# Spreading RMS-norm reciprocals with fp32 matmuls, summing the last squares on TensorE, and pairing two units tile by tile

## The reference

```python
mod = (silu(c) @ ada_w + ada_b).reshape(b, 9, 1024)        # shifts, scales and gates
h = modulate(rmsnorm(x, norm_ffn1_g), sh1, sc1)
x = x + 0.5 * g1 * swiglu(h, ffn1_w1, ffn1_w3, ffn1_w2)    # D_FF = 2816
h = modulate(rmsnorm(x, norm_mix_g), sh2, sc2)
xb, xc, xu, cq, ckv, kr = split(h @ w_in)
y_a = short_conv_mixer(xb, xc, xu, conv_w)
y_b = mla(cq, ckv, kr, ...)                                # norms of cq and ckv, 4 heads, 128x128 blocks
y = concat(group_rmsnorm(y_a, 8 groups), group_rmsnorm(y_b, 4 heads)) @ w_out
x = x + g2 * y
h = modulate(rmsnorm(x, norm_ffn2_g), sh3, sc3)
x = x + 0.5 * g3 * swiglu(h, ffn2_w1, ffn2_w3, ffn2_w2)
return rmsnorm(x, final_norm_g)
# rmsnorm(x, g) = x * rsqrt(mean(x * x) + EPS) * g
```

## Time and profile before

| what | value |
|---|---|
| runs of the kernel | 1052.28, 1052.82, 1054.54 us |
| span of the profiled execution | 1052.8 us; no further time of that execution is given |
| instructions | 13254 |
| mean granted TensorE clock | 0.974 |

### The profile page before, as it was taken

How to read it: one execution, slowest core, us unless ns; L and a number is a source line. 1 busy time by engine, 2 the same in 40 slices (tenths; PEclk the granted TensorE clock), 3 DMA queues, 4 the chain that set the end, 5 groups by cost and what they waited for, 6 DMA issues and landing times. The chain is left out here.

```text
span 1052.8 us, 13254 instructions
## 1 busy us (share of the span) xinstructions
PE 1009.5 (96%) x4505; PEld 831.4 (79%) x4505; DVE 564.9 (54%) x754; ACT 400.6 (38%) x568; POOL 66.3 (6%) x79
## 2 busy tenths in 40 slices
PE   3699999999999999999999989999999999999997
PEld 3678888888888888888867777788888888888886
DVE  5868777787753333754377645744434333333332
ACT  3254434444332222442255443353444444332222
POOL 2411111011000000000000310000000000000000
PEclk9599999999999999999999799999999999999999
DMA  9547766687633324123221101223323333333232
GB/s 333 175 133 249 242 198 211 206 256 235 202 92 93 92 90 115 50 81 100 80 65 40 41 23 58 80 80 100 98 85 96 99 100 100 94 93 93 90 109 81
DMA packets 176622, 127.82 MB, mean 121 GB/s; under 512 B 5069, under 2 KB 165718, under 8 KB 176598
## 3 DMA queue, kind: packets, MB, share of 16 engines
q1 hardware_dynamic: 168534, 98.14, 31.1%
q0 software_dynamic: 8064, 29.36, 8.4%
HBM read 125.39 MB, written 2.10 MB: 121 GB/s over the span
## 5 line engine op out<-in xcount | busy, mean ns | idle before, releaser
L722 PE MATMUL pb<-hh,wh 128*128 128x512 f32 x912 | 358.5, 393 | 5.0 <-DVE hl L1159 2.8
L722 PE MATMUL pb<-hh,wl 128*128 128x512 f32 x912 | 355.8, 390 | 0.0
L722 PE MATMUL pb<-hl,wh 128*128 128x512 f32 x912 | 355.7, 390 | 0.0
L1118 DVE TENSOR_TENSOR wl<-raw,wh 128x1024 fp32r<-128x1024 f32 x156 | 191.1, 1225 | 275.1 <-ACT wh L408 275.0
L408 ACT ACTIVATE wh<-raw 128x1024 fp32r<-128x1024 f32 x163 | 172.5, 1059 | 410.5 <-PE pb L722 410.5
L722 PEld LDWEIGHTS pb<-hh,wh 128*128 128x128 f32 x912 | 171.5, 188 | 46.5 <-DVE hl L1159 7.2
L722 PEld LDWEIGHTS pb<-hh,wl 128*128 128x128 f32 x912 | 171.6, 188 | 36.2
L722 PEld LDWEIGHTS pb<-hl,wh 128*128 128x128 f32 x912 | 171.7, 188 | 34.5
L722 PE MATMUL pb<-gh,wh 128*128 128x512 f32 x352 | 137.0, 389 | 0.0
L722 PE MATMUL pb<-gh,wl 128*128 128x512 f32 x352 | 136.9, 389 | 0.0
L722 PE MATMUL pb<-gl,wh 128*128 128x512 f32 x352 | 136.9, 389 | 0.0
(11 more groups left out here) (193 smaller groups left out, 763.2 us busy)
## 6 DMA issues: line engine op xcount, KB each, us to landing
raw<-in_ffn_w_dram SPq DMA_DIRECT2D x104, 512.0 KB, 3.8
ada_ring<-in_ada_w_dram POOLq DMA_DIRECT2D x56, 512.0 KB, 5.1
raw<-in_ffn_w_dram SPq DMA_DIRECT2D x32, 448.0 KB, 3.4
raw<-in_w_in_dram SPq DMA_DIRECT2D x17, 512.0 KB, 3.9
ada_start<-in_ada_w_dram SPq DMA_DIRECT2D x8, 1024.0 KB, 16.4
raw<-in_w_out_dram SPq DMA_DIRECT2D x8, 512.0 KB, 3.4
x_nat<-in_x_dram SPq DMA_DIRECT2D x1, 2048.0 KB, 10.5
out_dram<-o_nat SPq DMA_DIRECT2D x8, 256.0 KB, 2.9
```

The costliest lines, as they stand in the source:

```text
L722: last = pe.matmul(o, a, b, start=start and j == 0 and t == 0, stop=stop and j == len(pairs) - 1 and t == 2)
L1118: dve.tensor_tensor(wl[par][:, :], raw[par][:, :], wh[par][:, :].bitcast(F32), ALU.subtract).then_inc(lo_ready, 1)
```

## The change

Four things change. `inverse` only computes the reciprocals, after a wait until the spread before has been done (TensorE now reads `rrms` itself); the split parts, `diag` and their semaphores are gone. `norm_spread` is four fp32 matmuls, one for each column of reciprocals: the column, repeated 128 times, is the stationary operand and the identity is the moving one, 128 columns. For the norms of mix, FFN2 and the final one, `norm_sum_last` sums `sacc` of seven tiles and then the eighth square straight from its slot of `sq`, so that VectorE doesn't add it. `first_pair` uses each tile for both units at once. The filler counts change, and `fold` no longer waits for the first spread, since `turned` has its own place. The other lines renumber the count of additions (`ADD_BASE`).

```diff
-LAG = 3
-WARM_START, WARM_SQUARES, WARM_ROOT, WARM_NORMED, WARM_HEADS = 7, 16, 13, 16, 9
+WARM_START, WARM_SQUARES, WARM_ROOT, WARM_NORMED, WARM_HEADS = 7, 4, 3, 13, 9
...
+            def norm_sum_last(n, slot, applied):
+
+                pe.wait_ge(u_ready, applied)
+                pe.wait_ge(sq_added, ADD_BASE[n] + DT - 1)
+                for t in range(TT):
+                    pe.matmul(norm_bank[:, t:t + 1], cols(sacc, t), one_col, start=t == 0, stop=False, skip_group_check=True)
+                pe.wait_ge(sq_ready, SQ_BASE[n] + DT)
+                for t in range(TT):
+                    last = pe.matmul(norm_bank[:, t:t + 1], cols(sq[:, slot, :], t), one_col, start=False, stop=True, skip_group_check=True)
+                last.then_inc(col_done, 1)
...
             def norm_spread(n):
 
-                for part in range(2):
-                    pe.wait_ge(diag_ready, 2 * n + part + 1)
-                    last = pe.matmul(norm_bank[:, :], exact[:, 0, :], diag[:, part, :, :], start=part == 0, stop=part == 1)
+                pe.wait_ge(rrms_ready, n + 1)
+                for t in range(TT):
+                    last = pe.matmul(cols(norm_bank, t), rrms[:, t:t + 1].to_broadcast([P, P]), ident, start=True, stop=True)
                 last.then_inc(bc_done, 1)
...
-                for k in range(DT + LAG):
-                    for b, kb in ((0, k), (1, k - LAG)):
-                        if not 0 <= kb < DT:
-                            continue
-                        if kb == 0:
+                for k in range(DT):
+                    for b in range(2):
+                        if k == 0:
                             unit(base + b)
...
             warm(WARM_SQUARES)
-            pe.wait_ge(sq_added, SQ_BASE[N_MIX] + DT)
-            norm_sum(N_MIX, sacc, AP_BASE[N_MIX])
+            norm_sum_last(N_MIX, (SQ_BASE[N_MIX] + DT - 1) % 2, AP_BASE[N_MIX])
             warm(WARM_ROOT)
...
             def inverse(n, spread=True):
 
                 dve.wait_ge(rms_ready, n + 1)
+                if n >= 1:
+                    dve.wait_ge(bc_done, SPREAD[n] if spread else SPREAD[N_FFN2] + 1)
                 dve.reciprocal(rrms[:, :], rms[:, :]).then_inc(rrms_ready, 1)
-                dve.wait_ge(rrms_ready, n + 1)
                 if not spread:
-                    return
-                dve.tensor_copy(rrms_h[:, :], rrms[:, :]).then_inc(rrms_split, 1)
-                dve.wait_ge(rrms_split, 2 * n + 1)
-                dve.tensor_tensor(rrms_l[:, :], rrms[:, :], rrms_h[:, :].bitcast(F32), ALU.subtract).then_inc(rrms_split, 1)
-                if n >= 1:
-                    dve.wait_ge(bc_done, SPREAD[n])
-                idb = ident.unsqueeze(1).to_broadcast([P, TT, P])
-                for part, r in enumerate((rrms_h[:, :].bitcast(F32), rrms_l[:, :])):
-                    dve.wait_ge(rrms_split, 2 * n + part + 1)
-                    dve.tensor_tensor(diag[:, part, :, :], idb, r.unsqueeze(2).to_broadcast([P, TT, P]),
-                                      ALU.mult).then_inc(diag_ready, 1)
+                    dve.wait_ge(rrms_ready, n + 1)
```

More of the change, by code:

```diff
@@ L157, in hybrid_block @@
                                            ("group_rl", [P, SEQ], F32R))
-        diag_at = top[0]
-        diag = at("diag", [P, 2, TT, P], F32R)
-        (turned,), _ = place(diag_at, ("turned", [P, D_MODEL], F32))
+        turned = at("turned", [P, D_MODEL])
         region = top[0]
@@ L411, in landed, with square @@
                 return 16 * (n // 2 + 1)
-            def square(idx, slot, src):
-                if not isinstance(idx, int) or idx >= 2:
-                    act.wait_ge(sq_added, idx - 1)
+            def square(n, j, slot, src):
+                if n != N_FFN1 or j >= 2:
+                    act.wait_ge(sq_added, ADD_BASE[n] + j - 1)
                 act.activation(sq[:, slot, :], src, ACT.Square).then_inc(sq_ready, 1)
@@ L471, in _ @@
                 act.wait_ge(x_copied, k + 1)
-                square(k, k % 2, xres[:, k, :])
+                square(N_FFN1, k, k % 2, xres[:, k, :])
             sqrt_table(6)
@@ L507, in _ @@
                     act.wait_ge(zkv_copied, j + 1)
-                    square(SQ_BASE[N_KV] + j, (SQ_BASE[N_KV] + j) % 2, zkv[:, j, :])
+                    square(N_KV, j, (SQ_BASE[N_KV] + j) % 2, zkv[:, j, :])
                 elif j < KT + QT:
@@ L512, in _ @@
                     act.wait_ge(zq_copied, q + 1)
-                    square(SQ_BASE[N_Q] + q, (SQ_BASE[N_Q] + q) % 2, zq[:, q, :])
+                    square(N_Q, q, (SQ_BASE[N_Q] + q) % 2, zq[:, q, :])
                 if j == KT:
@@ L532, in conv_square @@
                 act.wait_ge(yc_ready, FREE + j + 1)
-                act.wait_ge(sq_added, SQ_BASE[N_Q] + QT)
+                act.wait_ge(sq_added, ADD_BASE[N_Q] + QT)
                 if j >= 2:
@@ L676, in _ @@
                         act.wait_ge(x_upd, DT + d + 1)
-                        square(SQ_BASE[N_FFN2] + d, (SQ_BASE[N_FFN2] + d) % 2, xres[:, d, :])
+                        square(N_FFN2, d, (SQ_BASE[N_FFN2] + d) % 2, xres[:, d, :])
                 if last:
@@ L757, in first_pair @@
             def first_pair(base, hbase):
[L759 to L763 removed]
+                for k in range(DT):
+                    for b in range(2):
+                        if k == 0:
                             unit(base + b)
[L765 to L768, removed]
+                        pe.wait_ge(hl_ready, hbase + k + 1)
+                        last = three(pb[b][:, :], [(cols(wh[b], k), cols(wl[b], k), hh[:, k, :], hl[:, k, :])],
+                                     k == 0, k == DT - 1)
+                        if k == DT - 1:
                             last.then_inc(unit_done, 1)
@@ L1079, in _ @@
             warm(WARM_SQUARES)
-            pe.wait_ge(sq_added, SQ_BASE[N_FFN2] + DT)
-            norm_sum(N_FFN2, sacc, AP_BASE[N_FFN2])
+            norm_sum_last(N_FFN2, (SQ_BASE[N_FFN2] + DT - 1) % 2, AP_BASE[N_FFN2])
             warm(WARM_ROOT)
@@ L1248, in update, with down_pair @@
                                          op0=ALU.mult, op1=ALU.add).then_inc(x_upd, 1)
-            def down_pair(base, f, n, upd, m, splits=6):
+            def down_pair(base, f, n, upd, m, splits=6, sums=2):
                 for s in range(6):
@@ L1255, in down_pair @@
                         update(d, 2 + p, half_gates[:, f, bass.ds(d, 1)], base + 6 * m + s + 1, upd)
-                        add_square(n, SQ_BASE[n] + 2 * m + p, (SQ_BASE[n] + p) % 2)
+                        if p < sums:
+                            add_square(n, 2 * m + p, (SQ_BASE[n] + p) % 2)
                     if s < splits:
@@ L1337, in _ @@
             clear_sum(N_MIX, N_FFN1)
-            with dve.Fori(0, DT // 2) as m:
+            with dve.Fori(0, DT // 2 - 1) as m:
                 down_pair(U_B1, 0, N_MIX, 0, m)
+            down_pair(U_B1, 0, N_MIX, 0, DT // 2 - 1, sums=1)
             inverse(N_MIX)
```

38 lines of the change are left out of this document (17 added, 21 removed).

## The result

The changed kernel took 1061.3 us (median of 1058.50, 1061.23, 1061.37 and 1061.41) against 1053.1 us for the kernel before (1052.28 to 1054.54, four runs): ratio 1.0074, 95% interval 1.0060 to 1.0088. It is 8 us slower. The forecast was 1053.1 with a range of 1049.0 to 1056.8, and the measured time lies 4.5 us beyond its upper end. The profiled execution is the one of 1058.50 us, its span 1056.8.

The account below looks back on a forecast made before the run. TensorE, busy 96% of the span, was taken as the bound. Terms -2.4 - 1.7 + 1.5 + 0.9 + 0.3 + 0 + 0 + 1.7 = +0.3 on 1052.8 gave 1053.1 us, range 1049.0 to 1056.8.

Parts of the forecast that it names:

- Second head, -2.4 - 1.7: Second head: without `diag` TensorE's stall goes, -2.4 us, and the half-clock stretch after it, another -1.7.
- Spreads, +1.5: KV, Q and heads: four fp32 matmuls cost TensorE 0.48 us more per spread in a stream, together +1.5 us.
- Last addition, mix 0: Mix norm: dropping the last addition gains 0, because `split_lo` of the next unit still holds the reciprocal.
- Final, +0.9: Final norm: two groups of sums stand behind the transposes in place of one, moving the end by +0.9 us.
- Start, +0.3: Kernel's start: half-clock spread replaces the `diag` wait, first tile at half clock for both units; +0.3 us.
- Clock at the norms, 0 and 0: Mix and FFN2 norms: fewer fillers let the clock fall, cancelling the shorter spread's gain; 0 us each.
- Pairs without lag, one fall, +1.7: First pairs: 0 by time, but TensorE's stands before unit 2 bring one clock fall among three places, +1.7 us.
- three falls: Rival: the clock falls behind all three first pairs, giving 1056.5 us; chance 0.22.
- The base: Starting time: the profiled execution's span of 1052.8 us was taken to stand for the runs' median of 1052.82.

Follow-up runs that it names:

- the changed kernel with the 64 bytes: Changed kernel plus 64 unused bytes a partition ahead of the region of `gh` and `gl`, restoring their old addresses; 1053.9 us, 1.0006 of the kernel before.
- bench1: Kernel before plus 512-column matmuls at varied operand addresses behind its last transposes; no total time given, final root at 1042.49 against 1044.22.

## Why the prediction was wrong

**The step that failed is one that it doesn't have.** The change frees `rrms_h` and `rrms_l`, and the prediction gives that no line. By moving `gh` and `gl` against the weights it costs 7.4 us, and 1053.1 + 7.4 = 1060.5 is within 1 us of what was measured. The forecast for the rest, without the addresses, was 1053.1; measured 1053.9. That is in part luck, since terms were missed on both sides; each is compared below, in the profile of the changed kernel with the 64 bytes against the profile of before.

- *Second head, -2.4 - 1.7*: right, -4.1 (reciprocal to reciprocal 10.53 us before, 6.45 here; the same with the spread alone). By the Trainium skill, "SBUF — State Buffer", section Who interferes with whom, a VectorE instruction with one SBUF input, outside the two-port modes, isn't held by GpSimd's; the trace agrees: in the changed kernel the reciprocal takes 0.18 us at 627.39, in the middle of a `wl` of GpSimd.
- *Spreads, +1.5*: right, 0.89 for 0.45 in a stream (forecast 0.93). By the Trainium skill, "FP8 and Floating Point Precision", section TensorE Precision Notes, true fp32 takes four passes; the estimate from that was 0.85 us, and the trace is 0.04 from it.
- *Last addition, mix 0*: right, `split_lo` bounds the reciprocal (423.69 against 423.82). *Final, +0.9*: right, 0.8.
- *Start, +0.3*: measured -0.2.
- *Clock at the norms, 0 and 0*: the mechanism was right at mix in this profile. The clock fell at 424.80, `ubuf` started 1.14 us earlier than before, 13 fillers took 4.04 us, and unit 0 was done at 439.23 against 439.25: nothing is left of the gain. At FFN2 it was mis-sized: unit 0 came 1.7 us later, since the second group of sums and the spread ran at half clock too (1.47 and 1.91 us). In the changed kernel's own profile the mix norm kept 1.00, and there 1.2 us were gained at `ubuf`. Of the four kernels with few fillers ahead of the sums one profile has the fall at mix (this one), and all four have it at FFN2 (3.4 us long in the two with the lag, 6.8 in the others).
- *Pairs without lag, one fall, +1.7*: mechanism and price of a fall right, the number too low. I gave three falls 0.22; the profiles have two here (1.7 and 1.4 us), three in the kernel before without lag, none in the changed kernel. By time the missing lag costs 0 to 0.3 us a pair where 0 was forecast.
- *Not foreseen*: in the first head the stretches at 0.50 are 10.2 us long in place of 17.1, and 1.6 us less are lost on the path. It isn't the length that counts: the spread alone and the pairs without lag, both on the kernel before, have 10.2 us too and gain nothing. These two have the fall early in the head (from 574.7 and 577.3) as before has (574.2), and this profile hasn't. As `bench1` hasn't it either, it takes no change for it to be missing; whether the change makes it rarer, these profiles don't tell.
- *The base*: a profiled execution's time is its span and 1.7 us (1058.50 for 1056.8, 1055.56 for 1053.9). That of before took some 1054.5, not 1052.8, so the prediction was wrong to let its span stand for the median. It joined the rows of an execution with a fall at 574, which `bench1` lacks, to the median of the others. The fall behind the second head, on which the -1.7 rests, is in every profile with `diag`.

## What to carry to other kernels

A deleted buffer is an edit to every address behind it: print both memory plans, compare them, and put a spacer in before anything else is judged. Where TensorE is the bound, check that moving and stationary operands have the same remainder by 256 (measured here for 512-column fp32r matmuls alone). Where a wait is shortened, shorten the fillers that were sized for it. Of a change that brings stands of 2 us in front of long matmul streams expect falls of the clock, whatever one profile shows; and before two profiles are compared, list the falls that each has.

## What was unexpected of the hardware

- The spacing of 512-column fp32r matmuls depends on the difference of their two operands' addresses by 256: 227 to 229 ns for 0, 229 to 230 for the moving one 64 ahead, some 232 to 235 for the other six steps of 32, with all other engines idle; 226.0, 228.2 and 232.7 in the down stages (the two windows by their 948 matmuls).
- The three stands of 1.8 to 2.3 us brought no, two or three falls of the clock in three profiles, each 3.4 us at 0.50 and worth 1.4 to 1.7.
- One and the same program had a fall of 3.4 us in its first head in one profile (574) and not in another, 1.7 us apart at the final root.
